# Neighbourhood attention in square query tiles: 640 keys in whole blocks instead of 768 or 832 in row bands

## The reference, cut to what matters

```python
z  = u_lat @ w_in                      # 1024 x 8192: B, C, X, G of the convolution branch, then q, k, v, gate of the attention
y_a = z_B * dwconv3(z_C * z_X) * silu(z_G)
for r in range(16):                    # rows of the grid
    rs = clip(r - 4, 0, 8)             # 8 rows of keys
    k_win, v_win = k[rs:rs+8, col_idx] # col_idx: 16 columns, start clip(c - 8, 0, 48)
    s_win = q_r . k_win + rpb[row - r + 7, col - c + 15]
    s_ctx = q_r . k_ctx                # 256 context keys
    p = softmax([s_win, s_ctx]);  y = p_win . v_win + p_ctx . v_ctx
y_lat = concat(y_a, y_b * silu(z_gate)) @ w_out
```

## Time and profile before

| what | value |
|---|---|
| time, median of 3 runs | 2731.02 us (2730.99 to 2731.94) |
| span of the profiled execution, first to last instruction | 2726.8 us |
| instructions | 35150 |
| TensorE busy | 2564.9 us (94%) |
| VectorE busy | 1652.5 us (61%) |
| ScalarE busy | 1248.6 us (46%) |
| GpSimd busy | 392.1 us (14%) |
| even layer: matmuls of L883 | 4608, from 75.3 to 1518.7 us |

### The profile page before, as it was taken

The page is one execution under the profiler, slowest core; times in us unless marked ns, Lnnn a source line. Parts: engine busy times, 40 slices in busy tenths (PEclk is TensorE's granted clock), DMA queues, the critical chain, the costliest instruction groups (busy, mean ns, idle before and its releaser), DMA issues. The chain is left out here.

```text
span 2726.8 us, 35150 instructions
## 1 busy us (share of the span) xinstructions
PE 2564.9 (94%) x12400; PEld 2187.7 (80%) x12400; DVE 1652.5 (61%) x2894; ACT 1248.6 (46%) x2026; POOL 392.1 (14%) x171
## 2 busy tenths in 40 slices
PE   6899999999999999999999889979999999997798
PEld 2888888878888888788888568868889888896687
DVE  5266566665666666656656563664776666765634
ACT  4333433434334334344343341435677666677422
POOL 1211111111111111111110020001111111111200
PEclk8999999999999999999999689989999999998899
DMA  5211110111112111112120165531111111112654
GB/s 218 70 39 41 57 47 26 57 55 41 65 34 65 39 34 57 47 34 74 40 64 16 72 205 153 169 93 39 46 62 39 38 62 46 62 39 93 209 152 149
DMA packets 153834, 200.84 MB, mean 74 GB/s; under 512 B 40544, under 2 KB 115424, under 8 KB 150624
## 3 DMA queue, kind: packets, MB, share of 16 engines
q1 hardware_dynamic: 110480, 167.02, 18.2%
q10 hardware_dynamic: 43072, 31.46, 4.2%
q0 software_dynamic: 144, 0.52, 0.1%
HBM read 167.00 MB, written 31.98 MB: 73 GB/s over the span
## 5 line engine op out<-in xcount | busy, mean ns | idle before, releaser
L883 PE MATMUL ps<-u_hi,w_hi 128*128 128x426 f32 (+1 forms) x1536 | 564.0, 367 | 16.6 <-POOL w_lo L539 16.6
L883 PE MATMUL ps<-u_lo,w_hi 128*128 128x426 f32 (+1 forms) x1536 | 548.9, 357 | 0.0
L883 PE MATMUL ps<-u_hi,w_lo 128*128 128x426 f32 (+1 forms) x1536 | 548.1, 357 | 0.0
L539 POOL TENSOR_TENSOR w_lo<-w_stage,w_hi 128x1024 fp32r<-128x1024 f32 x64 | 153.8, 2402 | 1196.0 <-ACT w_hi L586 1196.0
L883 PEld LDWEIGHTS ps<-u_hi,w_hi 128*128 128x128 f32 x1536 | 291.2, 190 | 26.1 <-POOL w_lo L539 16.7
L883 PEld LDWEIGHTS ps<-u_hi,w_lo 128*128 128x128 f32 x1536 | 290.8, 189 | 9.7
L883 PEld LDWEIGHTS ps<-u_lo,w_hi 128*128 128x128 f32 x1536 | 291.4, 190 | 8.1
L639 ACT ACTIVATE probs_t<-ps 128x768 fp32r<-128x768 f32 (+1 forms) x160 | 116.4, 727 | 316.2 <-PE ps L910 308.9
L1714 PE MATMUL ps<-u_hi,o_w_hi 128*128 128x426 f32 (+2 forms) x640 | 238.6, 373 | 13.9 <-POOL o_w_lo L1454 9.3
L1714 PE MATMUL ps<-u_hi,o_w_lo 128*128 128x426 f32 (+2 forms) x640 | 237.8, 371 | 0.0
L1714 PE MATMUL ps<-u_lo,o_w_hi 128*128 128x426 f32 (+2 forms) x640 | 237.7, 371 | 0.0
(11 more groups left out here) (182 smaller groups left out, 4715.7 us busy)
## 6 DMA issues: line engine op xcount, KB each, us to landing
y_tile<-y_scratch SPq DMA_DIRECT2D x72, 512.0 KB, 5.1
w_stage<-in_w_even SPq DMA_DIRECT2D x64, 512.0 KB, 3.4
o_w_raw<-in_w_odd SPq DMA_DIRECT2D x48, 512.0 KB, 3.4
ada_piece<-in_w_ada SPq DMA_DIRECT2D x16, 1024.0 KB, 5.6
wout_raw<-in_w_out SPq DMA_DIRECT2D x16, 1024.0 KB, 9.8
ada_pieces<-in_w_ada SPq DMA_DIRECT2D x4, 2048.0 KB, 18.2
bias_table<-in_bias_rows ACTq DMA_DIRECT2D x32, 256.0 KB, 4.4
y_scratch<-h_backward SPq DMA_DIRECT2D x16, 512.0 KB, 2.7
```

Of the source, the lines that this page charges most:

```text
L539: nc.gpsimd.tensor_tensor(wlo[:, slot, :], stage[:, slot, :], whi[:, slot, :].bitcast(F32), ALU.subtract).then_inc(w_lo, 1)
L883: last = nc.tensor.matmul(ps[:, bank(j, g), 0:t - f], w[:, slot, c * P:(c + 1) * P], x[:, c, f:t], start=(c == 0 and n == 0), stop=(c == K ...
```

## The change

- **Query tiles.** A latent tile is now 8 rows by 16 columns. Its keys are a block of 12 rows by 32 columns (384) in three blocks of 128, plus the context: 640 in 5 whole blocks for each tile. There are again 8 tiles a head (`top` 0 or 1, `ct` 0 to 3); the order is 4 tiles of head 0, 4 of head 1, for the upper half of the grid and then for the lower, and the context tiles of both heads come last. ScalarE writes Q, K and V reordered, K and V as (group of 4 rows, column, row in group), so that a window is three runs of 128.
- **Scores.** The low part of k now lies in `klo[:, h, :]` with 128 rows, the other 64 rows being zero, and is multiplied with the whole stacked q. `scores` waits for `neg_ready` in place of `exped`.
- **Softmax.** VectorE computes minus (score + bias) with its minimum in one pass over all keys, ScalarE one exponential with scale -1.
- **Bias.** GpSimd builds a tile of 384 for each step, two ahead, from a piece of 12 x 48 per query, loaded by SyncE's queue in 8 transfers per head and half of the grid, with the row mask added once per piece.
- **V.** 16 blocks of V are transposed per pair (overlapping windows) in place of 8.
- **Units.** Groups of 512, 512 and 256 columns. In the last pair units 0 to 7 stand in steps 0 to 7, and units 8 to 11 are cut in halves over steps 8 to 15.
- The result of the attention is written in place over `gate`; y is stored in two parts. The y buffer and the buffer of the tanh are gone. Semaphores of the output weights are shared by the two layers.

```diff
+EVEN_GROUPS = [(0, 512), (512, LAT), (LAT, TOK)]
+QROWS, QCOLS_TILE = 8, 16
+KROWS, KCOLS, KGROUP = 12, 32, 4
+KROW0 = [0, ROWS - KROWS]
+KCOL0 = [0, 8, 24, 32]
+WIN = KROWS * KCOLS
+KEYS = WIN + CTX
...
+    SPLIT_AFTER = {5: CB, 8: CG, 11: CQ, 14: CK}
+    LAT_STEPS = 2 * NLT
...
+    def pieces(s, last):
+        if not last:
+            return [(j, g, 0, KC) for j, g in (ORDER[s:s + 1] if s < STEPS - 1 else ORDER[s:])]
+        if s < 8:
+            return [(*ORDER[s], 0, KC)]
+        if s < LAT_STEPS:
+            return [(*ORDER[8 + (s - 8) // 2], s % 2 * (KC // 2), (s % 2 + 1) * (KC // 2))]
+        return []
...
+            def load_piece(q, head):
+                rows = a["bias_rows"]
+                top, slot = q // 2, q % 2
+                for r in range(QROWS):
+                    k0, k1 = (((0, 11), (0, 8)), ((4, 12), (0, 11)))[top][r // 4]
+                    at = r + k0 + (1, -3)[top]
+                    heads = bass.AP(tensor=rows.tensor, offset=at * P + GRID_W // 2,
+                                    ap=[[(TROWS + 1) * P, 2 * PAIRS], [1, 16], [P, k1 - k0], [1, TOE_COLS]])
+                    sp.dma_start(toe[16 * r:16 * r + 16, slot, k0:k1, :], heads[head]).then_inc(u_loaded[slot], 16)
+
+            def next_piece(i, q, last):
+                if q >= 2 and last:
+                    return
+                sp.wait_ge(t_ready, i * LAT_STEPS + (4 * q + 4))
+                load_piece((q + 2) % 4, 2 * i + (q % 2 + (2 if q >= 2 else 0)))
...
                 load_ada(i, 0)
-                for j in range(CX, CQ if last else CV + 3):
-                    sp.wait_ge(w_lo, i * 8 + (2 + j))
-                    load(chunk(i, j), (3 + j) % 2)
-                    if j == CG:
-                        load_ada(i, 1)
+                for j in (CX, CB, CG):
+                    load_w(i, j)
+                next_piece(i, 0, last)
+                if not last:
+                    load_w(i, CQ)
+                next_piece(i, 1, last)
...
+            def build_tile(i, n, slot_used=True):
+                h, top, ct = tile_of(n)
+                q = n // 4
+                piece = toe[:, h, :, :]
+                if ct == 0:
+                    pool.wait_ge(u_loaded[h], i * 256 + 128 * (q // 2 + 1))
+                    nc.gpsimd.tensor_tensor(piece, piece, rowm[:, top, :].unsqueeze(2).to_broadcast([P, KROWS, TOE_COLS]),
+                                            ALU.add).then_inc(u_masked, 1)
+                    pool.wait_ge(u_masked, i * 4 + (q + 1))
+                if slot_used:
+                    pool.wait_ge(neg_ready, i * STEPS + (n - 1 if n >= 2 else LAT_STEPS + n - 1 - STEPS))
+                j0 = KCOL0[ct] - QCOLS_TILE * ct + QCOLS_TILE
+                dst = table[:, n % 2, 0:WIN].rearrange("p (g c r) -> p g c r", c=KCOLS, r=KGROUP)
+                src = piece[:, :, j0:j0 + KCOLS].rearrange("p (g r) c -> p g c r", r=KGROUP)
+                col = colm[:, VARIANT[ct], :].unsqueeze(1).unsqueeze(3).to_broadcast([P, WIN // P, KCOLS, KGROUP])
+                nc.gpsimd.tensor_tensor(dst, src, col, ALU.add).then_inc(t_ready, 1)
...
-                if w:
-                    nc.scalar.activation(prob[:, b, 0:w], prob[:, b, 0:w], ACT.Exp, bias=negmax[:, b:b + 1],
-                                         accum_out=sums[:, b, 0:1])
-                nc.scalar.activation(prob[:, b, 576:832], ps[:, 3, 64:320], ACT.Exp, bias=negmax[:, b:b + 1],
-                                     accum_out=sums[:, b, 1:2]).then_inc(exped, 1)
+                nc.scalar.activation(prob[:, b, q], prob[:, b, q], ACT.Exp, scale=-1.0, bias=negmax[:, b:b + 1],
+                                     accum_out=sums[:, b:b + 1]).then_inc(exped, 1)
...
+            def row_max(i, s):
+                h, top, ct = tile_of(s)
+                b, q = s % 2, keys(s)
+                dve.wait_ge(scored, i * STEPS + (s + 1))
+                if top is not None:
+                    dve.wait_ge(t_ready, i * LAT_STEPS + (s + 1))
+                dve.sem_inc(row_ready, 1)
+                raw = ps[:, 2:4, :].rearrange("p a n -> p (a n)")[:, P + q.start:P + KEYS]
+                nc.vector.tensor_tensor_reduce(prob[:, b, q], raw, table[:, s % 2, q], -1.0, -NEG, ALU.add, ALU.min,
+                                               negmax[:, b:b + 1]).then_inc(neg_ready, 1)
...
             def scores(i, s):
...
-                pe.wait_ge(exped, i * STEPS + s)
+                pe.wait_ge(neg_ready, i * STEPS + s)
...
+                parts = [(ps[:, 3, 0:CTX], kst[:, h, LAT:TOK], klo[:, h, LAT:TOK])]
+                if top is not None:
+                    parts.append((ps[:, 2, P:512], window(kst, h, top, ct), window(klo, h, top, ct)))
+                for to, hi, lo in parts:
+                    nc.tensor.matmul(to, qst[:, h, q], hi, start=True, stop=False)
+                    last = nc.tensor.matmul(to, qst[:, h, q], lo, start=False, stop=True)
                 last.then_inc(scored, 1)
```

More of the change, by code:

```diff
@@ L142, in build_program @@
                          for layer in range(2)]
[L143 removed]
+        k["wout_loaded"] = [sem(f"wout_loaded{q}") for q in range(4)]
         k["odd_loaded"] = [sem(f"o_w_loaded{i}") for i in range(3)]
@@ L503, in load, with load_masks, mask @@
                 sp.dma_start(stage[:, slot, :], a["w_even"][g]).then_inc(w_loaded[slot], 16)
-            def prologue():
-                for dst, name in ((colmask, "colmask"), (rowmask, "rowmask"), (convw, "conv_a")):
-                    sp.dma_start(dst[:], a[name]).then_inc(s_const, 16)
+            def load_masks():
+                cols = a["colmask"]
+                def mask(dst, row, step, col, shift, n):
+                    lead = [[step, 8], [GRID_W, 16]] if step is not None else [[shift, 4], [0, 16]]
+                    src = bass.AP(tensor=cols.tensor, offset=row * GRID_W + col, ap=lead + [[1, n]])
+                    sp.dma_start(dst, src).then_inc(s_const, 16)
+                for v, ct in enumerate((0, 1, 3)):
+                    mask(colm[:, v, :], GRID_W - (ct + 1) * QCOLS_TILE, 0, KCOL0[ct], 0, KCOLS)
+                half = KROWS // 2
+                mid, at = GRID_W // 2 - 1, GRID_W // 2 - WIN_C // 2
+                for top in range(2):
+                    for r in range(2):
+                        q = slice(64 * r, 64 * r + 64)
+                        first, shift = (((at - 3, 1), (at, 0)), ((at - 4, 0), (at - 3, 1)))[top][r]
+                        mask(rowm[q, top, 0:half], mid, None, first, shift, half)
+                        mask(rowm[q, top, half:KROWS], mid, None, first + half + WIN_C - WIN_R, shift, half)
@@ L577, in _ @@
+                if not last:
+                    build_tile(i + 1, 0)
+                    build_tile(i + 1, 1)
+                    split_lo(chunk(i, CV), (3 + CV) % 2)
             run(pool, prologue, body)
@@ L685, in body @@
                         exp(i, s + 1)
-                    for j, g in step_unit(s, last):
-                        project(i, j, g, last)
+                    for j, g, c0, c1 in pieces(s, last):
+                        if c1 == KC:
+                            project(i, j, g, last)
                     copy_low(i, s)
@@ L856, in body @@
                         normalise(i, s + 1, link)
-                    for j, g in step_unit(s, last):
-                        project(i, j, g, link)
+                    for j, g, c0, c1 in pieces(s, last):
+                        if c1 == KC:
+                            project(i, j, g, link)
                     output(i, s, link)
@@ L942, in body, with prologue @@
                 ins.then_inc(v_turned, 1)
+            def prologue():
+                for j in (CQ, CK, CV):
+                    for g in range(NG):
+                        project(-1, j, g)
+                pe.wait_ge(zeros_set, 4)
+            def body(i, last):
+                turn_v(i)
                 project(i, BG, 0)
```

435 lines of the change are left out of this document (194 added, 241 removed).

## The result

| | median us | of 4 runs each |
|---|---|---|
| before | 2731.01 | 2722.06 to 2731.94 |
| after | 2474.47 | 2471.47 to 2475.02 |

The ratio is 0.9067, with a 95% interval of 0.9055 to 0.9078. The change takes 256.5 us off. The forecast was 2520, its range 2485 to 2605.

The account below looks back on a forecast made before the run. TensorE's queue was taken as the bound; 24.5 us saved in each of seven pairs (171.5), with 42.5 + 0.5 - 2 elsewhere, made 212.5 off the 2726.8 span, plus 4.2 around it: 2518.5, stated as 2520, range 2485 to 2605.

Parts of the forecast that it names:

- V +0.9: V transposes on TensorE: 16 in place of 8 add 0.9 us a pair.
- The row change: Attention matmuls: each switch between 128 and 64 contraction rows leaves some 0.2 us of weight load exposed on TensorE.
- rival C: SP's queue: bias pieces arrive late, making the kernel slower, about 2850 us at 55 us a piece; chance 3%.
- 3 us of stalls a pair: TensorE waiting on the softmax chain in steps after the change: 3 us a pair, against 3.8 read from the trace.
- the cover of the short step: Step with a 256-column projection: the softmax chain needs 3.6 of 4.0 us, leaving 0.4 us spare.
- the +0.5 that the sum takes: Sum for a pair: 0.5 us of saving added to 27.5 less 3.5, giving 24.5.
- TensorE is idle 2.2 where it was 0.2: Start of a pair, before the first turn: longer idle, then a low clock losing 1.3 to 1.7 us; together 3.5 lost.
- The forecast's pair of 158.8: Steady pair after the change: 183.3 us shortened by 24.5; the stated sign was 157 to 161 us.
- -42.5: Eighth, last pair: 129.5 us for 172.0, with the softmax chain deciding steps 8 to 15.
- the +2: Output weights loaded after the last projection: about 17 us remain for 4 MB, costing 2 us, range 0 to 6.
- the forecast's 4.2: Time around the span: the median run of 2731.0 us was 4.2 longer than the profiled span of 2726.8.
- a turn at the early end: Start of a pair: first turn put 0.5 us later, at 19.0, with ends from -1.0 to +2.9 us.

Follow-up runs that it names:

- low64: Changed kernel with the low part of K multiplied over its own 64 rows again instead of 128 with zeros: 2564.6 us.
- nohalves: Changed kernel with the last pair's units 8 to 11 whole in steps 8 to 11, none in steps 12 to 19: 2480.4 us.
- tinytile: Changed kernel with GpSimd's 16 tile additions a pair cut to 4 elements a row: 2475.9 us.
- b_tinytable: Kernel before with GpSimd's four bias table additions a pair cut to 4 elements a row: 2703.7 us.
- b_groups: Kernel before with projection groups of 512, 512 and 256 columns in the even layer: 2698.9 us.
- b_low128: Kernel before with the second scores matmul over all 128 rows, using the high part of K in place of the low: 2650.4 us.
- b_keys384: Kernel before with 384 latent keys in every latent tile, the other 128 or 192 left out: 2623.5 us.

## Why the prediction came out 45 us too high

**Right.** TensorE's queue set the time in the pairs, and what left it left the span. Each priced part of it stands: weigh 0.59 (0.59), scores 0.59 (0.58), projections 112.4 us a pair for 114.2 (-1.8 for the forecast's -1.9), V +0.9. The maximum took 0.823 us (0.83), turn_lo 0.820 (0.82). The row change was the cause (low64). The halves help the last pair (nohalves +5.9). The bias pieces and tiles came in time (tinytile; no wait on them in the pair's timeline), so rival C fell, with 1.12 us for a tile add, inside its bounds.

**The step that failed: "so I count 3 us of stalls a pair, where the trace has 29.2 us in all of them, 3.8 a pair".** Three things were wrong with it. The group's idle time was spread over eight pairs, while the last held 16 of the 29 and a steady pair 1.9: a row for the whole span was read as a rate per pair. The 1.9 were then carried over as if a property of the schedule, and they had a maker, the long table adds, which the change takes out; b_tinytable ends them, and so do, for 12 of 13 us, the groups of b_groups, which the change has too. And the cover of the short step was put at 0.4 where it is 0.7 to 0.9. Measured in a steady pair of after: 0.0 before weigh. Two slips beside it are small: 29.2 over eight pairs is 3.65, not 3.8, and the +0.5 that the sum takes is the difference to 3 by neither.

**The other part of it: "TensorE is idle 2.2 where it was 0.2 ... followed here by about 3 us at a granted clock of 0.58".** The first turn came at 18.4 for 19.0, after an idle of 0.88, and the clock stayed at 1.00. One stretch of before with a low clock had been made a rule for every idle of that size. The seven pairs of before have seven equal waits of 1.21 to 1.28 us, and the low clock followed three of them. What decides it is not shown: none of after's waits of 1.36 to 1.54 was followed by it, but in low64 and b_groups one jump each was (waits of 1.84 and 1.83 us, then 3.4 us of low clock from 451.0 and 477.1).

By size: count as work the distances between TensorE's starts, idle time left out, and take what the low clock adds as lost. A pair of before is then 179.5 of work and 3.8 lost (3.0 idle, 0.8 by the low clock). A pair of after is 151.6 of work and 2.3 lost, of which 1.3 on average are the wait at the loop's jump, which nobody had forecast. The work that leaves is 27.9 for the forecast's 27.5. The forecast's pair of 158.8 had 152.0 of work and 6.8 lost, where 2.3 were measured. So 34.5 of the 45.5 us are 7 x (0.4 + 4.5), with rounding.

The rest: last pair -45.0 for -42.5, the first pair's start 0.9 earlier, the output weights without the +2 and the rest of that stretch 1.9 shorter, 2.2 less around the span, and 1.5 by which 2520 was rounded up. Of the 2.2: each timed run on record is 1.8 us longer than its own span, and by this the profiled execution of before was 2.4 us faster than the median, which the forecast's 4.2 took in.

Both large errors were allowances for trouble that stayed away. The range was narrower than its own terms. With no stalls (3 us a pair less), a turn at the early end (1.5 less) and no low clock (1.5 less), seven pairs take 42 us off 2520; that estimate is 2478, below the stated 2485.

**The parts on the kernel before** give -78, -106, -30 and -12, together -226 of -257. b_low128 and b_keys384 each left waits for the softmax, which the one-pass maximum and single exponential take away. TensorE's idle time in the seven pairs is 27 us above that of before in the one and 7 in the other, near the missing 31. But the shorter softmax was not run alone on the kernel before, so that it makes the 31 is argued, not shown. It stays open, too, how much of b_groups's 15 us of vanished stalls (12 of waits before weigh, some 4 by the low clock, others less, against 6 more at the jump) is a longer cover and how much a shift of the table adds against VectorE.

## What to carry to other kernels

Where TensorE is the bound, look at the starts of neighbouring matmuls with different numbers of contraction rows: filling the shorter ones with zeros can pay although it adds work (here 90 us). Before an idle time of the page is carried over to the changed kernel, split it by stage with a window, and find which instruction makes it; ask whether the change takes that one out. When TensorE's step gets shorter, shorten the softmax chain of other engines with it, or the saving turns into waits.

## What the runs showed of the hardware

- Four score matmuls and five transposes take 1.26 + 0.53 us when two of the four run over 64 contraction rows, 0.59 + 0.47 when all run over 128: 0.73 us for four changes of rows, some 0.2 each, with loads of nearly equal length (183 and 187 ns). The loads of other rows start 0.21 to 0.37 us after the matmul ahead instead of with it (low64, after).
- A loop's jump leaves TensorE idle 1.36 to 1.54 us in after, where the last unit is 256 columns wide. Where it was 426, the idle time at that place was 0.5 on average, and ScalarE's copy of V ended it. Six jumps written out give back 8.4 us.
- Seven equal waits of 1.21 to 1.28 us in before were followed by the low clock three times, for 3.4, 3.4 and 6.8 us; waits of 0.9 and 1.4 us in after never were (clock 1.00 through all seven pairs).
- pv_out has two operands in SBUF and takes 0.28 us alone and 1.74 beside a GpSimd add of 2.41, while turn_lo, which reads PSUM and SBUF, kept to 0.82 beside a tile add of 1.11 (after, 615.9 to 621.6). The Trainium skill ("SBUF — State Buffer", section Terms) has that the two engines share a pair of ports, held for the full instruction; the trace agrees for pv_out, which ended 0.14 us after the add.
